# Fetching every second value block by a GpSimd gather of 128 rows instead of a SyncE transfer

## What is computed

```python
def peer_ffn(x, w_q, sub_keys, u, v):
    ...
        gates = jax.nn.softmax(cand_s, axis=-1)
        ue = jnp.take(u, experts, axis=0)
        ve = jnp.take(v, experts, axis=0)
        act = jax.nn.gelu(jnp.einsum('chkd,cd->chk', ue, xc), approximate=False)
        return jnp.einsum('chk,chkd->cd', gates.astype(xc.dtype) * act, ve)
```

## Time and profile before

| | |
|---|---|
| median of 3 runs | 4001.96 us (4001.95 to 4002.72) |
| the profiled execution | 4003.63 us |
| its span, first to last instruction | 4001.80 us |
| mean granted clock of TensorE, as a share of full speed | 0.986 |
| busy: PE, PEld, DVE, ACT, POOL | 97%, 81%, 59%, 39%, 40% |
| the two value stages | about 1290 to 1981 us and 3282 to 3976 us |
| loads of `peer_v` in both layers | 256, of 512 KB each |

### The profile page before, as it was taken

How to read it: one execution, slowest core, us unless ns; L and a number is a source line. 1 busy time by engine, 2 the same in 40 slices (tenths; PEclk the granted TensorE clock), 3 DMA queues, 4 the chain that set the end, 5 groups by cost and what they waited for, 6 DMA issues and landing times.

```text
span 4001.8 us, 67766 instructions
## 1 busy us (share of the span) xinstructions
PE 3890.5 (97%) x19488; PEld 3249.9 (81%) x19488; DVE 2370.9 (59%) x4680; ACT 1549.2 (39%) x2412; POOL 1600.3 (40%) x1044
## 2 busy tenths in 40 slices
PE   8998999999999999999899989999999999999997
PEld 8877888878887888888798778888788878888886
DVE  1555088887776555555625541888877765555555
ACT  2453344445554322223224523444455543222232
POOL 3433144447776222222243432444577752222222
PEclk9999999999999999999999999999999999999998
DMA  4001234436775555555420012444367755555553
GB/s 151 11 1 59 84 134 141 142 128 179 200 201 172 182 177 179 184 180 183 172 86 10 2 68 82 141 142 142 126 187 201 201 169 182 177 180 184 180 184 129
DMA packets 394527, 563.53 MB, mean 141 GB/s; under 512 B 220000, under 2 KB 253536, under 8 KB 390496
## 3 DMA queue, kind: packets, MB, share of 16 engines
q1 hardware_dynamic: 197088, 512.39, 37.8%
q10 hardware_dynamic: 197376, 50.33, 6.2%
HBM read 443.10 MB, written 119.54 MB: 141 GB/s over the span
## 4 chain that ended last, share of the span: by engine, by line
PE 95%; issue 2%; DVE 1%; POOL 1%; ACT 0%; DMA 0%; DVEq 0%; SPq 0%; ACTq 0%; POOLq 0%
PE ps L1476 35%; PE ps L1209 16%; PE ps L1210 16%; PE ps L1211 16%; PE ps L1447 3%; PE ps L1331 3%; PE ps L1308 2%; PE ps L1316 2%; PE ps L1297 1%; PE ps L1404 1%; PE ps L1281 0%; PE ps L1286 0%; DVE x_tok L1036 0%; DMA w_raw<-in_w_in 0%; POOL w_lo L419 0%
## 5 line engine op out<-in xcount | busy, mean ns | idle before, releaser
L562 POOL TENSOR_TENSOR st_lo<-st_raw,st_hi 128x1024 fp32r<-128x1024 f32 x400 | 966.1, 2415 | 1905.6 <-ACT st_hi L714 1905.6
L1209 PE MATMUL ps<-t_hi,st_hi 128*128 128x512 f32 x2304 | 911.8, 396 | 1.8 <-DVE t_lo L856 1.3
L1210 PE MATMUL ps<-t_lo,st_hi 128*128 128x512 f32 x2304 | 908.9, 395 | 0.0
L1211 PE MATMUL ps<-t_hi,st_lo 128*128 128x512 f32 x2304 | 908.4, 394 | 0.0
L714 ACT CAST st_hi<-st_raw 128x1024 fp32r<-128x1024 f32 x544 | 569.7, 1047 | 706.3 <-PE ps L1476 706.3
L1476 PE MATMUL ps<-st_hi,wt_hi 128*128 128x512 f32 x2048 | 630.9, 389 | 0.0
L1476 PE MATMUL ps<-st_lo,wt_hi 128*128 128x512 f32 x2048 | 630.5, 389 | 0.0
L1476 PE MATMUL ps<-st_hi,wt_lo 128*128 128x512 f32 x2048 | 630.4, 389 | 0.0
L1170 DVE TENSOR_TENSOR wt_lo<-w_f,wt_hi 128x512 fp32r<-128x512 f32 x256 | 400.5, 1565 | 342.4 <-ACT wt_hi L822 342.4
L1211 PEld LDWEIGHTS ps<-t_hi,st_lo 128*128 128x128 f32 x2304 | 431.6, 187 | 107.2
L1209 PEld LDWEIGHTS ps<-t_hi,st_hi 128*128 128x128 f32 x2304 | 432.3, 188 | 103.2 <-DVE t_lo L856 1.8
(11 more groups left out here) (174 smaller groups left out, 4708.1 us busy)
## 6 DMA issues: line engine op xcount, KB each, us to landing
st_raw<-in_peer_u SPq DMA_DIRECT2D x256, 512.0 KB, 3.3
st_raw<-in_peer_v SPq DMA_DIRECT2D x256, 512.0 KB, 3.5
gelu_d<-h_out SPq DMA_DIRECT2D x256, 256.0 KB, 2.2
h_in<-gelu_d SPq DMA_DIRECT2D x256, 256.0 KB, 3.6
gates_d<-g_stage ACTq DMA_DIRECT2D x48, 1024.0 KB, 7.3
g_in<-gates_d SPq DMA_DIRECT2D x256, 192.0 KB, 3.4
w_raw<-in_w_in SPq DMA_DIRECT2D x16, 1168.0 KB, 5.2
st_raw<-in_peer_w_q SPq DMA_DIRECT2D x32, 512.0 KB, 3.3
```

The costliest lines, as they stand in the source:

```text
L562: nc.gpsimd.tensor_tensor(st_lo[:, s].rearrange("p c f -> p (c f)"), st_raw[:, s], st_hi[:, s].rearrange("p c f -> p (c f)").bitcast(F32), ...
L1209: nc.tensor.matmul(dst, lhs[0], rhs[0], start=first, stop=False)
L1210: nc.tensor.matmul(dst, lhs[0], rhs[1], start=False, stop=False)
L1211: return nc.tensor.matmul(dst, lhs[1], rhs[0], start=False, stop=last)
```

## The change

One new tile `v_row` holds a row number for each of the 128 partitions. POOL fills it once at the start with 128 + partition, and adds 256 in each pass of the value loop, and once more at the end of a layer. All rows of `peer_v` of both layers are seen as one table of rows of 1024 numbers. In each of the 63 passes POOL, before its subtraction, starts a gather that puts row `v_row[p]` of this table on partition `p` of `st_raw` half 1, and that adds 16 to the new semaphore `s_vrow` when it has landed. SP leaves these 63 loads of a layer out. ACT waits for `s_vrow` instead of `s_straw[1]` in this loop, and elsewhere its count of `s_straw[1]` is made smaller to match. The bytes moved, the buffers and the work of PE and DVE are the same.

```diff
@@ the value loop of SP
             with sp.Fori(1, EB // 2) as i:
                 for s in range(2):
-                    st_load(i + (QB + EB) // 2, s, a["peer_v"][l, 2 * i + s])
+                    if s == 0:
+                        st_load(i + (QB + EB) // 2, s, a["peer_v"][l, 2 * i + s])
                     gated_load(i, s)
@@ the start of POOL's program
         pool.sem_inc(g_sum, RING)
+        nc.gpsimd.iota(v_row[:], [[0, 1]], base=P, channel_multiplier=1).then_inc(row_set, 1)
+        pool.wait_ge(row_set, 1)
@@ POOL, the value loop
-            with pool.Fori((QB + EB) // 2 + 1, ST_PER // 2) as m:
-                rest_block(m, 1)
+            v_rows_all = a["peer_v"].rearrange("l b p d -> (l b p) d")
+            with pool.Fori(0, EB // 2 - 1) as i:
+                nc.gpsimd.tensor_scalar(v_row[:], v_row[:], 2.0 * P, None, ALU.add).then_inc(row_set, 1)
+                pool.wait_ge(st_l[1], ST_PER // 2 * l + (QB + EB) // 2 + i + 1 + 1)
+                pool.sem_inc(waited, 1)
+                pool.wait_ge(row_set, EB // 2 * l + i + 1 + 1)
+                pool.sem_inc(waited, 1)
+                nc.gpsimd.indirect_dma_start(
+                    out=st_raw[:, 1], out_offset=None, in_=v_rows_all,
+                    in_offset=bass.IndirectOffsetOnAxis(ap=v_row[:, 0:1], axis=0)).then_inc(s_vrow, 16)
+                rest_block(i + (QB + EB) // 2 + 1, 1)
+            nc.gpsimd.tensor_scalar(v_row[:], v_row[:], 2.0 * P, None, ALU.add).then_inc(row_set, 1)
             norm_tail(1)
@@ ACT, round_block
-            def round_block(m, s):
+            def round_block(m, s, landed=None):
 
-                act.wait_ge(s_straw[s], (ST_PER // 2 * l + m + 1) * 16)
+                if landed is not None:
+                    act.wait_ge(s_vrow, ((EB // 2 - 1) * l + landed + 1) * 16)
+                elif s == 0:
+                    act.wait_ge(s_straw[0], (ST_PER // 2 * l + m + 1) * 16)
+                else:
+                    act.wait_ge(s_straw[1], ((ST_PER // 2 - EB // 2 + 1) * l + m + 1) * 16)
                 act.wait_ge(st_used, ST_PER * l + 2 * m + s + 1)
@@ ACT, the value loop
                     round_gated(2 * i + s + 1, 1 - s)
-                    round_block(i + (QB + EB) // 2 + 1, s)
+                    round_block(i + (QB + EB) // 2 + 1, s, landed=i if s else None)
```

More of the change, by code:

```diff
@@ L160, in build @@
     warm = keep.tile("warm", [P, 1], F32)
+    v_row = keep.tile("v_row", [P, 1], U32)
     att = Region(keep.end)
@@ L299, in build @@
     eq_ready = sem("eq_ready")
+    row_set, s_vrow = sem("row_set"), sem("s_vrow")
     wt_f, wt_h, wt_l = sem("wt_f"), sem("wt_h"), sem("wt_l")
```

## The result

| | median of the runs | lowest to highest | runs | profiled execution | its span |
|---|---|---|---|---|---|
| before | 4002.19 us | 3999.64 to 4003.58 | 14 | 4003.63 us | 4001.8 us |
| changed | 4010.66 us | 4004.14 to 4014.86 | 14 | 4009.04 us | 4007.0 us |

What follows compares the result with a forecast made beforehand. The value stage was taken to be bound by PE's matmuls, with the gather hidden in slack. Added 0, removed 0 left the span at 4001.8 and the median at 4002 us; hidden alone spans 3999 to 4005, the range stretched up to 4100.

Steps and rivals of the forecast that it cites:

- The case with 0.74: Value stage: POOL's new work and the gather stay hidden under PE's matmuls, median 4002 us; chance 0.74.
- The hidden case: Value stage: gather lands 0.6 us before ACT's cast, nothing added; 4002 us, alone spanning 3999 to 4005; chance 0.74.
- ring-bound case: Value loop: E above 2.97 us makes the buffer ring set the pace; 4288 at E 5.24, first part 4097; chance 0.11.
- SP's issue, ACT's wait: Value loop: SP's remaining half 1 loads go out 4.6 us earlier, ACT waits on another semaphore with 1.71 us idle; 0.
- The start: POOL in the value loop: gather starts 0.89 us after its subtraction ends, including 0.10 increment and 0.24 semaphore.
- E: Time in which POOL makes the gather's 128 row transfers, taken as 2.39 us, between 0.33 and 5.24.
- The threshold: Weight buffer ring must close within 10.88 us, leaving E 2.97 us; each further 0.1 us costs 12.6 us.
- Exclusion: POOL and DVE keep each other out of SBUF in the value loop, data 1.3 us late, +165: 4167; chance 0.06.
- Row by row: Gather on POOL: each row number handled by itself, E 12.5 us, period 20.4, +1203: 5205; chance 0.05.
- Not spread: Gather: all rows go through one DMA engine, 512 KB takes 25 us, total well over 6000; chance 0.02.
- the iota ... 0: Program start: the iota stands before a POOL instruction that begins after 15.06 us idle, so it costs 0.

Runs made afterwards that it cites:

- fill1: Changed kernel with one memset of 128x1024 on POOL ahead of each gather; 4011.33 us, ratio 1.0025.
- fill4: Changed kernel with four memsets of 128x1024 on POOL, one after the other, ahead of every gather; 4459.14 us, ratio 1.114.
- two_issues: Changed kernel with a second, small transfer (128 rows of 256 bytes) issued by POOL ahead of each gather; 4024.85 us, ratio 1.0062.
- tile_only: Kernel before with the new tile v_row in keep, used by no instruction, later tiles 64 bytes further on; 4008.47 us, ratio 1.0016.
- gather_free: Changed kernel, gather included, with v_row in free bytes so that no other tile moves; 4004.77 us, ratio 1.0009.
- rows_only: Kernel before with the new tile, iota, increments and their waits on POOL, but SP loading every block, no gather; 4006.85 us, ratio 1.0011.
- plain_pool: Changed kernel with a plain transfer of the same block issued by POOL in the gather's place; 4007.82 us, ratio 1.0014.
- row_early: Changed kernel with the increment made ahead of POOL's subtraction, once the last gather has landed; 4009.16 us, ratio 1.0016.
- gather_128: Changed kernel with v_row 128 bytes wide instead of 4, so later tiles lie 128 bytes higher instead of 64; 3996.25 us, ratio 0.9988.

## Why the prediction was right, and where it wasn't

The case with 0.74 held in its mechanism for the value stage: it stays bound by PE, POOL's new work lies under it, and no rival came. But the sum was 0 and the kernel lost 8.5 us, so the median of 4002 was missed by as much as is needed to tell two kernels apart here. The hidden case had 3999 to 4005 for itself; 4010.66 lies above it, and within the range only because that was stretched to 4100 for the first part of the ring-bound case, which didn't come. That the range held is luck. Step by step:

*SP's issue, ACT's wait: 0, and right.* SP's issues for half 1 go out 4.5 us earlier (1649.79, against 1653.54 moved by the 0.73 us between the two periods), predicted 4.6. ACT's idle time is 1.72 us, ended by PE.

*The start: 0.89 predicted, 1.44 measured.* The increment was right: it was to be held by DVE's subtraction until 1653.26 and done 0.10 us later, and moved by the 0.73 us between the two periods that is 1654.09, where 1654.08 was measured (alone it takes 0.21 us, not 0.10, but it begins while DVE is still at work). The term that failed is the 0.24 us from there to the gather, taken from a semaphore that releases SP: it was 0.81, and fill1 shows that 0.16 would do for a memset, so that the rest belongs to the DMA instruction.

*E: 2.39 predicted, 1.04 measured,* and 4.2 us from the gather's start to its landing against my 5.9. The fit of the Trainium skill ("DMA: Bandwidth & Descriptors", Anatomy of one DMA) gave 3.2: a plain transfer took 3.8 and the gather 4.2, so both were off, and the fit less. The start was 0.6 us too early and the landing took 1.7 us less than assumed, so the block lands 1.7 us before the cast at 1660.80, and not 0.6.

*The threshold.* Sound, by fill4's rows, whose terms add up to its period. But it holds one term that isn't a constant: the landing is 4.2 us while PE binds and 5.1 to 5.5 once the gather runs on top of SP's load. With 5.4 the changed kernel's ring is 1.05 + 0.09 + 2.39 + 1.44 + 5.4 = 10.4 us: 0.5 us is the true slack, enough to recover from one late gather in two passes; with 0.72 us more on POOL (two_issues) it is gone.

*The rivals.* Ring-bound didn't come (E 1.04 against 2.97). Exclusion cost nothing: DVE holds up the increment, as assumed, but not the gather, and DVE's mean of line 1190 is 1569 ns against 1565 before (line 1170). Row by row didn't: 12.5 us expected by it, 1.04 measured; the rule of the Trainium skill ("GPSIMD Engine Reference", Performance pitfalls) of some 102 cycles for each index, an estimate of 10.9 us, doesn't describe this instruction. Not spread neither: the block lands in 4.2 us, where one engine was to take 25.

*What no step held.* Two things. First, the edit was followed through the queues and not through memory: in "the iota ... 0" the tile that the iota writes was costed with its instruction, and that the tile moves all others wasn't asked. Its price is 6.3 us by tile_only's median. The rows needed were in the trace of before: DVE's copy at 512.33 and POOL's subtraction at 512.35 are a tie, and e_all at 862.56 with PE's transpose at 863.3 has no slack behind it. Second, the gather's price was taken from one period and multiplied; that one of 126 could start 2.8 us late was not asked, and 2.5 us follow by gather_free's median (1.8 in its profiled execution).

What stays open: why PE runs at 1073, 1077 or 1094 matmuls in 250 us with the same clock, how the place of the tiles enters into it, and what holds the 114th transfer. The slip isn't fixed by the layout alone. With the tiles 64 bytes up, six of eight profiled executions slipped (changed, rows_only, fill1, tile_only, two_issues, fill4; not plain_pool and row_early), and the two that didn't were the fastest of eleven runs each; with no tile moved none of 4 did. The changed kernel's 14 runs fall into two groups: three at 4004 to 4006 us, the others at 4009 and more. That the copy takes 2.54 us when POOL is first is shown by the rows; which displacement gives which arrival was only tried at 0, 64 and 128 bytes.

## What to carry to other kernels

A new tile costs more than its bytes: place it where nothing else moves, or time the kernel before with the tile alone, or the change will be charged with (or praised for) what the placement did, here from +6.3 to -6.5 us. In a kernel whose engines run in step, look for pairs of instructions on engines that hold each other up and that start within a few hundredths of a microsecond, as 512.33 and 512.35 here; they are where an unrelated edit shows. A ring of buffers needs slack not only for the usual transfer but for the rare late one, and it must be large enough to win the time back, since a long wait of PE can cost clock on top of itself (gather_128).

## What the runs showed of the hardware that was not expected

- A gather of 128 rows of 4 KB keeps POOL for 1.04 us, a plain transfer of the same block 0.62 us; they land 4.2 and 3.8 us after their start, SP's own 3.5.
- The 114th transfer that POOL issues starts 2.3 to 2.8 us late, plain or by row numbers; with two a pass the 114th and the 226th.
- A tensor_scalar of 128x1 uint32 takes POOL 0.21 us by itself (row_early) and 0.57 us where a DVE subtraction with both inputs in SBUF runs beside it (changed). A memset that waits for it starts 0.16 us after its end, a DMA instruction 0.6 to 0.8 us. A memset of 128x1024 takes 0.95.
- A displacement of the tiles behind `keep` by 64 or 128 bytes changed the kernel by +6.3 and -6.5 us, and PE's time for a matmul in one stage from 233 to 228.5 ns at the same granted clock.
- After PE had waited 3.9 us (gather_128) its granted clock was 0.50 for the next 5 us, with 12 matmuls in place of 24.
